# Half-size filler groups, dilated products three steps behind, early triangular masks added in PSUM, and a first gate tile among the first block-sparse groups

## What is computed

```
h = rms_norm(x, g_pre);  proj = h @ w_in             # q/k/v of both attentions, gate logits
o_a = dilated_attention(...)   # 3 groups of 4 heads: (window, dilation) = (128,1), (512,4), (2048,16)
o_b = moba_attention(...)      # 4 heads, causal, blocks of 256, own block + top-3 past blocks
merged = sigmoid(gate_a) * (o_a @ w_br_dil) + sigmoid(gate_b) * (o_b @ w_br_moba)
x = x + rms_norm(merged @ w_out, g_post)
a = causal_dwconv3(h2 @ w_gate) + conv_b
x = x + rms_norm((gelu(a) * (h2 @ w_up)) @ w_down, g_post2)
```

## Time and profile before

| | us |
|---|---|
| median of 3 runs | 3966.84 |
| the profiled execution | 3966.89 |
| its span, slowest core (5) | 3965.6 |
| spans of the 8 cores | 3959.4 to 3965.6 |
| granted TensorE clock | 0.992 to 0.994 |
| TensorE busy | 3821.5 (96%) |
| VectorE, ScalarE, GpSimd busy | 2079.8, 1868.8, 876.1 |

### The profile page before, as it was taken

One profiled execution on the slowest core, in us unless ns is written; L12 is line 12 of the kernel. 1 busy time (PEld: TensorE's weight loads), 2 busy tenths in 40 slices (PEclk: granted clock), 3 DMA queues, 4 the chain that ended last, 5 costly groups with the idle time before them and its releaser, 6 DMA issues.

```text
span 3965.6 us, 57672 instructions; the slowest of 8 cores (3959.4 to 3965.6 us)
## 1 busy us (share of the span) xinstructions
PE 3821.5 (96%) x20656; PEld 1859.7 (47%) x20656; DVE 2079.8 (52%) x3265; ACT 1868.8 (47%) x3653; POOL 876.1 (22%) x1484
## 2 busy tenths in 40 slices
PE   6989999999998999999999899999999989999999
PEld 4544444444554444444465344444446534444444
DVE  4454566455346456636435645664643564565363
ACT  3456355354345635535434554553533465465251
POOL 2331232111132133211113213221111322222110
PEclk9999999999999999999999999999999999999999
DMA  6132668344213367745432246783432225567341
GB/s 144 28 72 51 138 148 153 93 92 84 65 33 63 54 141 151 143 138 91 102 91 40 56 72 134 159 144 101 75 85 49 52 47 92 135 145 132 108 73 69
DMA packets 185600, 381.09 MB, mean 96 GB/s; under 512 B 32288, under 2 KB 48928, under 8 KB 185312
## 3 DMA queue, kind: packets, MB, share of 16 engines
q0 software_dynamic: 118656, 190.89, 31.3%
q1 hardware_dynamic: 66672, 186.51, 14.5%
HBM read 500.52 MB, written 67.63 MB: 143 GB/s over the span
## 4 chain that ended last, share of the span: by engine, by line
PE 90%; DVE 5%; ACT 3%; issue 1%; POOL 0%; DMA 0%; SPq 0%; DVEq 0%; POOLq 0%; ACTq 0%
PE psum L379 54%; PE psum L1252 15%; PE psum L537 6%; PE psum L608 5%; PE psum L660 5%; PE psum L939 3%; PE psum L685 2%; PE psum L487 1%; ACT s_arena L947 1%; DVE s_arena L781 1%; DVE s_arena L698 1%; DVE s_arena L371 0%; DVE s_hb L467 0%; ACT s_hb L458 0%; DMA s_xr<-x 0%
## 5 line engine op out<-in xcount | busy, mean ns | idle before, releaser
L379 PE MATMUL psum<-s_hT,s_slabs 128*128 128x512 bf16 x9728 | 2187.3, 379 | 7.5 <-DVE s_arena L1212 2.1
L379 PEld LDWEIGHTS psum<-s_hT,s_slabs 128*128 128x128 bf16 x9728 | 937.0, 98 | 1095.2 <-issue 25.3
L1252 PE MATMUL psum<-s_arena 128*128 128x512 bf16 x2816 | 615.0, 379 | 0.0
L1201 DVE SCALAR_TENSOR_TENSOR s_arena<-s_arena,s_convw 128x512 f32<-128x512 f32 x352 | 264.2, 751 | 434.8 <-ACT s_arena L1193 434.4
L1252 PEld LDWEIGHTS psum<-s_arena 128*128 128x128 bf16 x2816 | 274.1, 98 | 323.6
L660 PE MATMUL psum<-s_arena 128*128 128x128 bf16 (+2 forms) x1840 | 354.3, 268 | 63.3 <-DVE s_arena L951 21.2
L427 DVE SCALAR_TENSOR_TENSOR s_tz<-psum,s_stat,s_gpost 128x1024 f32<-128x1024 f32 x128 | 164.1, 1282 | 421.3 <-POOL s_stat L406 421.3
L947 ACT ACTIVATE s_arena<-psum 128x512 bf16<-128x512 f32 (+3 forms) x640 | 296.4, 550 | 72.3 <-PE psum L939 60.5
L175 POOL DMA_DIRECT2D s_slabs<-w_in_r x224 | 122.6, 550 | 908.1 <-PE psum L660 454.0
L698 DVE TENSOR_TENSOR s_arena<-s_arena,s_dmask 128x512 bf16<-128x512 bf16 (+1 forms) x384 | 192.1, 504 | 218.3 <-ACT s_arena L693 216.7
L1192 ACT COPY s_arena<-psum 128x512 f32<-128x512 f32 x352 | 205.6, 584 | 197.3 <-PE psum L379 197.3
(11 more groups left out here) (72 smaller groups left out, 3522.6 us busy)
## 6 DMA issues: line engine op xcount, KB each, us to landing
s_slabs<-w_in_r POOLq DMA_DIRECT2D x224, 256.0 KB, 4.5
xs<-s_xr SPq DMA_DIRECT2D x96, 512.0 KB, 3.5
s_xr<-xs SPq DMA_DIRECT2D x96, 512.0 KB, 4.6
s_slabs<-w_gate_r POOLq DMA_DIRECT2D x176, 256.0 KB, 3.9
s_slabs<-w_up_r POOLq DMA_DIRECT2D x176, 256.0 KB, 4.8
s_xr<-x SPq DMA_DIRECT2D x64, 512.0 KB, 5.6
s_arena<-w_down POOLq DMA_DIRECT2D x88, 256.0 KB, 6.0
y<-s_xr SPq DMA_DIRECT2D x32, 512.0 KB, 3.0
```

Of the source, the lines that this page charges most:

```text
L379: inst = nc.tensor.matmul(out, lhsT=l_, rhs=r_, start=(i == 0), stop=(i == n - 1))
L1201: d1 = DVE.do(nc.vector.scalar_tensor_tensor(out=t1_, in0=a_[:, 1 + 512 * tgi:513 + 512 * tgi], scalar=convw[:, l, fc, 1:2], in1=t1_, op0= ...
L1252: inst = nc.tensor.matmul(ps[zb + n], lhsT=uT[:, kc, i * 128:(i + 1) * 128], rhs=wdn[kc][:, n * 512:(n + 1) * 512], start=(kc == 0), stop= ...
```

## The change

Four edits, all in the mixer:

1. `proj_fm` and the gate groups write their eight products in two halves with a yield of 0.87 after each. `mm_group` is unchanged and remains in use elsewhere.
2. `dil_unit` has SKEW = 3.
3. In blocks of query groups 0 and 1 (32 of the 64 diagonal units of a mixer), the mask becomes a second product into the same bank: the identity times `ntri`, a constant that holds -30000 above the diagonal, over 128 columns. The exponential gives zero there, and VectorE's multiplication is left out in these units.
4. The filler of the block-sparse stretch is split in two. `side` (block choice, division of the dilated result) and `fill_pe` run beside each other, each at ratio 1.25. In `fill_pe` the last projection is stretched by 1.5, and the gate products and Tanh of the first chunk follow at once, stretched by 3.4, into four buffers of their own (`AB0`); their branch products wait until `ready()`. The delays of the division of the first four blocks shrink from 6, 16, 6, 16 units to 5, 12, 5, 12.

Inside `gates` the loop body is now two generators, `gate_mm` (products and Tanh) and `branch_mm` (branch products and VectorE's three operations). The weight buffers of a gate chunk are also released after its gate products, before its branch products.

```diff
-def merge(main, fill, ratio):
+def merge(main, *fills):
+    live = [[gen, ratio, 0.0] for gen, ratio in fills]
     for cost in main:
...
+        for f in list(live):
+            f[2] += cost * f[1]
+            while f[2] > 0:
+                try:
+                    f[2] -= next(f[0])
...
+def scaled(gen, factor):
+    for cost in gen:
+        yield cost * factor
+def pause(cost):
+    for _ in range(int(2 * cost)):
+        yield 0.5
...
@@ proj_fm @@
-                tp = mm_group(ps[b], [(buf[:, kc * 128:(kc + 1) * 128], hT[:, kc, tg * 512:(tg + 1) * 512]) for kc in range(8)],
-                              [tokw, hT_tok[4 * tg:4 * tg + 4]])
+                PE.wait(tokw, hT_tok[4 * tg:4 * tg + 4])
+                inst = None
+                for kc in range(8):
+                    inst = nc.tensor.matmul(ps[b], lhsT=buf[:, kc * 128:(kc + 1) * 128], rhs=hT[:, kc, tg * 512:(tg + 1) * 512],
+                                            start=(kc == 0), stop=(kc == 7))
+                    if kc == 3:
+                        yield 0.87
...
-                yield 1.75
+                yield 0.87
@@ dil_unit @@
-            SKEW = 2
+            SKEW = 3
@@ moba @@
-                todo.append([16 if k < 4 else 28, lambda: norm_mult(k, qg, pair, rt)])
-                todo.append([6 if k < 4 else 10, bcast])
+                todo.append([12 if k < 4 else 28, lambda: norm_mult(k, qg, pair, rt)])
+                todo.append([5 if k < 4 else 10, bcast])
...
-                todo.append([6 if k < 4 else 10, gather])
-                todo.append([16 if k < 4 else 24, lambda: norm_recip(k, qg, pair, tl)])
+                todo.append([5 if k < 4 else 10, gather])
+                todo.append([12 if k < 4 else 24, lambda: norm_recip(k, qg, pair, tl)])
...
+                    diag = kt >= 4 * qg
+                    pe_mask = diag and qg < 2
+                    inst = nc.tensor.matmul(ps[bS][:, 0:nq], lhsT=Kx[:, kt * 128:(kt + 1) * 128],
+                                            rhs=Qx[:, qg * 512 + c0:(qg + 1) * 512], start=True, stop=not pe_mask)
+                    if pe_mask:
+                        inst = nc.tensor.matmul(ps[bS][:, 0:128], lhsT=identb[:, :], rhs=ntri[:, :], start=False, stop=True)
...
-                    if kt >= 4 * qg:
+                    if diag and not pe_mask:
                         DVE.wait(tE)
@@ gates @@
+                bufs, e_wait, factor, ready = early
+                for tgi in range(2):
+                    yield from scaled(gate_mm(0, tgi, bufs, e_wait), factor)
+                while not ready():
+                    yield 0.5
+                for tgi in range(2):
+                    yield from branch_mm(0, tgi, bufs)
+                first = 1
@@ mixer @@
-                yield from par(chain(mqk_proj(l, 1, 0, w1, mq[1], FB2), gating(1, mq[1], aug_t[1], sel[1], FB2)),
-                               gating(0, mq[0], aug_t[0], sel[0], FB2), dil_den(1, m_wait, nt1))
-                while not all((q, p) in done for q in range(2) for p in range(2)):
-                    yield 0.5
-                yield from gates(l, 0, nt1, ob_done, FB2, nt1, mts, wout_load)
-            merge(moba(mq, aug_t, sel, vt[3], done, m_wait, on_p0), fill_m(), 1.25)
+            def fill_pe():
+                yield from scaled(mqk_proj(l, 1, 0, w1, mq[1], FB2), 1.5)
+                yield from gates(l, 0, nt1, ob_done, FB2, nt1, mts, wout_load, (AB0, nt0, 3.4, ready))
+            side = par(chain(pause(8.0), gating(1, mq[1], aug_t[1], sel[1], FB2)),
+                       gating(0, mq[0], aug_t[0], sel[0], FB2), dil_den(1, m_wait, nt1))
+            merge(moba(mq, aug_t, sel, vt[3], done, m_wait, on_p0), (side, 1.25), (fill_pe(), 1.25))
```

More of the change, by code:

```diff
@@ L574, in build @@
         AB = [carve((12 + 2 * i) * KB, 512) for i in range(4)]
+        AB0 = [carve((60 + 2 * i) * KB, 512) for i in range(4)]
         uT = carve(0, 11264, BF16).rearrange("p (c t) -> p c t", c=NFC)
@@ L1297, in qk_tg @@
                     next(gen)
+                    next(gen)
                 yield
@@ L1408, in _constants @@
         "tri": tri.astype(bf),
+        "ntri": ((1.0 - tri) * NEG).astype(bf),
         "qaug_t": qaug_b, "kaug_t": kaug_b,
```

134 lines of the change are left out of this document (70 added, 64 removed).

## The result

The changed kernel is slower, by little. It took 3992.48 and 3994.27 us; the kernel before took 3966.92 us as the median of 6. The ratio is **1.0063, 95% interval 1.0046 to 1.0081**, so some 25 us more where 47 us less were forecast, and outside the range (3892 to 3950 us). In four of six executions of the changed kernel the cores of a die ran slower at a lower clock (its plain median is 4116.1 us), so all times and ratios here rest on the executions in which none did. The profiled execution spans 3991.0 us against 3965.6 us.

A forecast was written before the change was run, and what follows sets the result against it. TensorE, busy 96% of the span, was taken as the bound, with time only in its holes. From 3966.9 us, -19 (dilated) and -28 (block-sparse, masks included) gave 3920 us; range 3892 to 3950 us.

The forecast's parts named there:

- rival C: Block-sparse stretch: with shorter delays VectorE stands for late division DMAs and product banks come late; 74 us, 3994 us; chance 0.06.
- So 7.3 - 2.6 = 4.7 us per mixer go: Dilated units: half groups and SKEW = 3 remove all waits but those at unit ends; -19 us over four mixers.
- for banks that ScalarE copies out: Dilated products with V: 7.2 us of their 29.4 us of waits over four mixers, counted among those to be covered.
- I assume the same: End of dilated unit (1,1): the stall of 1.31 us read at the end of (2,1) was taken there too.
- Splitting the groups elsewhere costs nothing: Filler outside the dilated gaps: half groups cost no time, since the same products follow each other.
- The price of a mask product: Block-sparse query groups 0 and 1: 0.056 us each, 128 in all, +7 us; far bound 30 us.
- rival B: ScalarE is the limit: waits for masks become waits for exponentials; -20 us, 3946 us; chance 0.22.
- the stretch to the first branch product: From the first block-sparse score to the gates' first branch product: some 51 us per mixer, clock above 0.95.
- 28 forecast: Block-sparse edits, masks included: -7.1 us per mixer, -28 us in all.
- R = 10: TensorE time in us still lost per mixer in the block-sparse stretch up to the gates, against 18.9 before.
- A: All of it is hidden: loss falls to 5 us per mixer, clock full, unit ends shrink; -74 us, 3892 us; chance 0.12.
- D: The change does not do what it says: half groups land where full ones did; 3960 us; chance 0.02.

The follow-up runs named there:

- e4: The kernel before with SKEW = 3 in the dilated units alone, full filler groups: 3957.7 us, ratio 0.9969.
- e3: The kernel before with the filler projections cut into half groups alone, SKEW still 2: 3954.2 us, ratio 0.9968.
- e8: The changed kernel with two loads of w_out per call of wout_load and the old division delays (6, 16, 6, 16 units): 3932.9 us, ratio 0.9913.
- e12: The changed kernel without GpSimd's additions of the second and third dilated groups to the first: 3975.5 us in its one execution that counts.
- e13: The kernel before without GpSimd's additions of the second and third dilated groups to the first: ratio 1.0007.

## Why the prediction was wrong

**The step that failed by omission: the loads written by gate tile, +40 us.** The prediction said what an earlier gate start frees, not what is paced by it. GpSimd's queue it never went through. The price could be counted in the kernel and its trace: eight loads, one per tile, eight tiles left instead of eleven, and 17 us between the last issue and its first reader in the kernel before, of which the fewer tiles take 9.4 and the place behind the next weights takes 7.

**"Against it: 12 units of about 0.6 us are 7 us, above 5.8" (rival C), +18 us.** The mechanism was named with its place and given a chance of 0.06 as a rival to the forecast, when it was a term of it. The sum compared means; the chain has two waits in the queue of VectorE, and 57.0 us of standing against 14.4 show that 12 units don't cover them each time. The rival's own count was off as well: it priced all 32 chains, but only the first four blocks of a mixer have shorter delays, which are 16. The 18 us are 1.1 us for each of these, and alone they would not have turned a gain of 47 us; with the load the sign turned. That rival C's 3994 us lie 2 us from the measured time is luck: its price was 74 us, and most of what was lost instead is the load. Nor do its two DMA trips bear out a fixed price of some 2 us each: in the chain of the earlier trace rows they take 1.4 and 3.5 us from issue to landing.

**"So 7.3 - 2.6 = 4.7 us per mixer go" (dilated), 1.8 instead, +12 us.** Either half of the change alone gave 3.0 to 4.4 (e4, e3). The 7.2 us of waits "for banks that ScalarE copies out" were added up as going, and they are what grew, from 21 late starts and 10.8 us to 60 and 19.6; the waits for masks and for the reductions of K did go. "I assume the same" for the unit's end was wrong too, since the stall at the end of (2,1) grew from 1.31 us to 2.17. "Splitting the groups elsewhere costs nothing" was not contradicted (e3).

**What held.** The price of a mask product, 0.05 us against the 0.056 forecast; no wait for ScalarE's exponentials of the size of rival B (L961 behind L972: 3.3 us over the whole span). Of the stretch to the first branch product the size came near: 55.4 us (270.8 to 326.16) and 53.1 to 54.6 in the other mixers where the sum had 51, at clocks of 0.94 to 1.00 where it had above 0.95. And once the load and the delays are mended (e8), block-sparse stretch and rest together are 4 x 2.7 + 21.1 = 32 us shorter than before, against 28 forecast; with the 7 us of the dilated part, less some 2 us at the start, this is e8's 36 us of span. In part that is luck. In e8 the stretch to the first branch product takes 56.7 us on average with 44.1 us of work in it (the sum's 40.6 and the 3.5 that its longer delays leave there), so 12.6 are lost where the forecast had R = 10; what makes up for it came behind that place, where the forecast had nothing.

So 3920 lacks 40 (load), 18 (delays) and 12 (dilated) us: 3990 against 3992 measured. Load and delays are differences of timed runs, the dilated part is read from the stages, so that the sum closes to 2 us says little about each term.

Of the rivals, A, B and D are out. The chances by size (within 2%: 0.95) were borne out; the sign was not.

## What to carry to other kernels

When work is moved or a stage starts earlier, list everything that is issued by that stage's progress, DMAs first, and compare the time from the last issue to its first reader before and after with the landing time in the trace. Look also at what stands ahead of these DMAs in the list of the engine that issues them. Delays ahead of a DMA's reader on an engine that works in order are slack for all that is queued behind it, and shortening them has to be argued from the longest chain, not the mean. Two remedies for one wait are to be timed alone and together.

## What the runs showed of the hardware

VectorE and GpSimd got into each other's way: a VectorE product of two SBUF tensors (128x256, 16-bit) takes 0.29 us on average without GpSimd's additions (e12, e13), 0.47 with them in the kernel before and 0.61 in the changed one, and one that started while an addition ran took 1.65; GpSimd's additions took 1.5 to 1.6 us each. The Trainium skill (page "SBUF — State Buffer", section "SBUF: two separate sides") says that the two engines share a pair of ports as an exclusive lock, held for a whole instruction, when VectorE reads two SBUF inputs and GpSimd reads SBUF. The mask that ends at 270.19, just behind an addition that ends at 270.04, agrees with it.

After 8.4 us without products TensorE ran at half rate for 3.8 us: nine products, 0.43 us apart against 0.216, at a granted clock of 0.50. A late transfer costs its wait and that: 34.5 and 8.2 us over four mixers. The 256 KB loads of `w_out` in the changed kernel took 4.0 to 11.3 us from issue to landing.

A wait that a trace records as short can cost more than it shows: the 60 waits for ScalarE's bank copies have 10.8 us of recorded idle time, and their products start 19.6 us late.
